# Seven products of 256 columns in place of eight for the three feed-forward parts

## The reference, cut to what matters

```python
def swiglu_ffn(x, w_gate, w_up, w_down):
    return (jax.nn.silu(x @ w_gate) * (x @ w_up)) @ w_down
...
        x = layer_norm(DN_ALPHA * x + 0.5 * swiglu_ffn(x, ffn1_wg[i], ffn1_wu[i], ffn1_wd[i]),
                       ln1_g[i], ln1_b[i])
...
        h = rmsnorm(x, norm_mlp_w[l]) * (1.0 + scale2) + shift2
        x = x + gate2 * (jnp.square(jax.nn.relu(h @ w_up[l])) @ w_down[l])
```

## Time and profile before

| | |
|---|---|
| three runs, median | 5414.38 us |
| profiled execution | 5398.97 us, span 5397.2 us, mean granted clock 0.969 |
| TensorE busy | 5041.7 us, 93% |
| VectorE busy | 1668.1 us, 31% |
| ScalarE busy | 872.1 us, 16% |
| matmuls of the pairs (line 261) | 3465.9 us busy, 8016 records |
| weight loads of the same | 1524.9 us busy |

### The profile page before, as it was taken

One profiled execution on the slowest core, in us unless ns is written; L12 is line 12 of the kernel. 1 busy time (PEld: TensorE's weight loads), 2 busy tenths in 40 slices (PEclk: granted clock), 3 DMA queues, 4 the chain that ended last, 5 costly groups with the idle time before them and its releaser, 6 DMA issues.

```text
span 5397.2 us, 48490 instructions
## 1 busy us (share of the span) xinstructions
PE 5041.7 (93%) x21092; PEld 2886.4 (53%) x21092; DVE 1668.1 (31%) x2883; ACT 872.1 (16%) x1483; POOL 146.7 (3%) x228
## 2 busy tenths in 40 slices
PE   8999997989999998999999999899999788888988
PEld 3444444775564443466555444344444677778843
DVE  1211875440211001462442100221010555555501
ACT  0001023121021000311221100010001333233211
POOL 0000000000000000000000000000000111111000
PEclk9999998999999999899999999999999899999999
DMA  5432441003222222111111222222221000000021
GB/s 199 150 111 53 70 66 45 1 3 92 86 79 70 72 78 68 47 39 63 39 41 54 68 73 78 70 70 70 71 69 56 3 1 1 1 1 1 17 89 39
DMA packets 284883, 311.14 MB, mean 58 GB/s; under 512 B 7168, under 2 KB 277632, under 8 KB 281472
## 3 DMA queue, kind: packets, MB, share of 16 engines
q1 hardware_dynamic: 284672, 308.04, 19.2%
HBM read 305.92 MB, written 2.10 MB: 57 GB/s over the span
## 4 chain that ended last, share of the span: by engine, by line
PE 51%; DVE 3%; ACT 2%; issue 0%; DMA 0%; SPq 0%; DVEq 0%; ACTq 0%
PE ps L261 31%; PE ps L579 4%; PE ps L592 2%; PE ps L566 1%; PE ps L2417 1%; PE ps L1727 1%; PE ps L306 1%; PE ps L342 1%; PE ps L2435 1%; PE ps L599 1%; PE ps L2656 1%; PE ps L1446 1%; PE ps L2178 1%; PE ps L1435 1%; PE ps L2348 0%; PE ps L2337 0%
## 5 line engine op out<-in xcount | busy, mean ns | idle before, releaser
L261 PE MATMUL ps<-main,w 128*128 128x512 f32 (+1 forms) x8016 | 3465.9, 593 | 69.6 <-DMA w<-in_ffn_wg 19.0
L261 PEld LDWEIGHTS ps<-main,w 128*128 128x128 f32 x8016 | 1524.9, 191 | 1933.6 <-issue 1905.6
L579 PE MATMUL ps<-main,w 128*128 128x128 f32 x1536 | 219.3, 290 | 4.3 <-DVE main L2521 2.5
L579 PEld LDWEIGHTS ps<-main,w 128*128 128x128 f32 x1536 | 197.2, 201 | 16.5 <-issue 6.8
L535 DVE SCALAR_TENSOR_TENSOR main<-main,ps 128x512 f32<-128x512 f32 x44 | 30.3, 688 | 553.0 <-PE ps L261 553.0
L592 PE MATMUL ps<-main 128*128 128x128 f32 x1440 | 195.6, 292 | 2.4 <-DVE main L638 2.4
L488 DVE SCALAR_TENSOR_TENSOR main<-main,params_sb 128x512 f32<-128x512 f32 x256 | 192.5, 752 | 9.1
L592 PEld LDWEIGHTS ps<-main 128*128 128x128 f32 x1440 | 184.4, 207 | 10.6 <-issue 7.5
L612 ACT COPY main<-ps 128x512 f32<-128x512 f32 x180 | 105.5, 586 | 516.4 <-PE ps L566 516.4
L566 PE MATMUL ps<-consts_sb,main 128*128 128x128 f32 x944 | 141.1, 276 | 7.0 <-DVE main L622 7.0
L546 DVE SCALAR_TENSOR_TENSOR main<-main,ps 128x512 f32<-128x512 f32 x32 | 22.0, 688 | 399.9 <-PE ps L261 399.9
(11 more groups left out here) (417 smaller groups left out, 3853.6 us busy)
## 6 DMA issues: line engine op xcount, KB each, us to landing
w<-in_w_in SPq DMA_DIRECT2D x58, 1024.0 KB, 6.5
w<-in_e_w_in SPq DMA_DIRECT2D x28, 1024.0 KB, 5.0
main<-in_ada_w SPq DMA_DIRECT2D x24, 1024.0 KB, 9.3
w<-in_ffn_wg SPq DMA_DIRECT2D x22, 1024.0 KB, 5.2
w<-in_ffn_wu SPq DMA_DIRECT2D x22, 1024.0 KB, 5.3
w<-in_o_w_in SPq DMA_DIRECT2D x20, 1024.0 KB, 5.4
w<-in_ffn_wd SPq DMA_DIRECT2D x16, 1024.0 KB, 4.8
w<-in_w_up SPq DMA_DIRECT2D x16, 1024.0 KB, 5.4
```

Of the source, the lines that this page charges most:

```text
L261: i = pe.mm(PS[b][:, 0:n], wv[:, k, f * 128:(f + 1) * 128], g.X(kg + k), start=kg + k == 0, stop=kg + k == g.nk - 1)
L579: t = pe.mm(one(PS[b], i), one(MT, i), one(Dm, i), start=True, stop=True)
```

## The change

The three parts use the scheme of Strassen in Winograd's form. A pair of output features by a pair of inner tiles is a 2x2 block matrix of 128x128 weights, and two inner tiles by two halves of the tokens a 2x2 block matrix of 128x256 data. Instead of eight block products of 256 columns (done before as four of 512) there are seven, each summed over the n = 4 pairs of inner tiles of one weight buffer (n = 3 in the last group of the ffn's down). What is multiplied and how the results are combined needs sums:

- four sums of weights for each buffer, two steps ahead (`dve_seven_weights`), in two sets of buffers;
- four sums of data for each pair of inner tiles, once for x and once for the hidden tiles (`dve_halves`, three instructions each);
- four instructions on the results of each step (`dve_seven_out`), out of four banks, beside one copy by ScalarE.

A step is now one weight buffer: the down products are no longer summed in PSUM over all inner tiles, but added to X step by step. The first pair of gate and of the MLP's up stays as it was. Silu runs on two tiles at once in SBUF, the MLP's ReLU and square are one instruction of VectorE. The modulation rows have three buffers rather than seven and stand one behind each step (three behind the first). U2 has one set of 16 tiles.

```diff
     w_landed = [ctx.enter_context(nc.semaphore(f"w_landed{i}")) for i in range(4)]
-    mod_landed = [ctx.enter_context(nc.semaphore(f"mod_landed{i}")) for i in range(7)]
     PS = [ctx.enter_context(nc.psum_tensor(f"ps{i}", [128, 512], F32))[:, :] for i in range(8)]
-    banks, weights = Turns(8), Turns(4)
...
+    def seven_room(g, j, kg):
+        n, (S, first, _, _) = min(8, g.nk - kg) // 2, g.seven
+        w = wbuf[weights.of.get((g, j, kg), 0)][:, 0:n * 512].rearrange("p (m e f n) -> p m e f n", e=2, f=2, n=128)
+        i = sets.of.get((g.name, j, kg), 0)
+        parts = [S[i](q)[:, 0:n * 128].rearrange("p (m n) -> p m n", n=128) for q in range(4)]
+        return n, [[w[:, :, e, f, :] for e in range(2)] for f in range(2)], parts, first[i]
+    def pe_seven(pe, g, j, kg=0):
+        step = (g.name, j, kg)
+        weights.take(g, j, kg)
+        sets.take(*step)
+        n, w, S, _ = seven_room(g, j, kg)
+        _, _, XS, key = g.seven
+        into = [banks.take("seven", i, *step) for i in range(4)]
+        def product(q, i, half, weight, x):
+            b, before = into[i]
+            if before:
+                pe.wait_ge(*at("out", *before))
+            for m in range(n):
+                t = pe.mm(PS[b][:, 256 * half:256 * half + 256], weight[:, m, :], x(m), start=m == 0, stop=m == n - 1)
+            t.then_inc(pe.inc(sem["pe", "dense"], "mm", f"seven {q}", *step), 1)
...
+        def own(e, half):
+            return lambda m: g.X(kg + 2 * m + e)[:, 256 * half:256 * half + 256]
+        def sums(q):
+            return lambda m: XS[kg // 2 + m][q // 2][:, 256 * (q % 2):256 * (q % 2) + 256]
...
+        pe.wait_ge(*at("w", g.name, j, kg))
+        for m in range(0, 2 * n, 2):
+            pe.wait_ge(*at(*g.ready, kg + m))
+        product(1, 0, 0, w[0][0], own(0, 0))
+        yield
+        for m in range(1, 2 * n, 2):
+            pe.wait_ge(*at(*g.ready, kg + m))
+        product(2, 1, 0, w[0][1], own(1, 0))
+        yield
+        for m in range(n):
+            pe.wait_ge(*at("halves", *key, kg // 2 + m))
+        product(4, 3, 1, w[1][1], sums(3))
+        yield
+        pe.wait_ge(*at("sums", *step))
+        product(6, 1, 1, S[1], sums(2))
+        pe.also("w used", *step)
+        yield
+        product(5, 2, 0, S[0], sums(0))
+        yield
+        product(7, 2, 1, S[2], sums(1))
+        yield
+        product(3, 3, 0, S[3], own(1, 1))
+        yield
+    def act_seven(a, g, j, kg=0):
+        step = (g.name, j, kg)
+        before = sets.before.get(step)
+        if before:
+            a.wait_ge(*at("out", "seven", 1, *before))
+        a.wait_ge(*at("mm", "seven 1", *step))
+        _, _, _, first = seven_room(g, j, kg)
+        a.copy(first, bank("seven", 0, *step)[:, 0:256]).then_inc(
+            a.inc(sem["act", "dense"], "out", "seven", 0, *step), 1)
+    def dve_seven_weights(v, g, j, kg=0):
+        s, step = sem["dve", "dense"], (g.name, j, kg)
+        before = sets.before.get(step)
+        if before:
+            v.wait_ge(*at("mm", "seven 3", *before))
+        v.wait_ge(*at("w", *step))
+        _, ((a11, a12), (a21, a22)), S, _ = seven_room(g, j, kg)
+        v.tt(S[0], a21, a22, ADD).then_inc(v.inc(s, "sum 0", *step), 1)
+        v.tt(S[2], a21, a11, SUB).then_inc(v.inc(s, "sum 2", *step), 1)
+        v.wait_ge(*at("sum 2", *step))
+        v.tt(S[1], S[2], a22, ADD).then_inc(v.inc(s, "sum 1", *step), 1)
+        v.wait_ge(*at("sum 1", *step))
+        v.tt(S[3], a12, S[1], SUB).then_inc(v.inc(s, "sums", *step), 1)
+    def dve_halves(v, key, X, XS, m, ready):
+        s = sem["dve", "dense"]
+        x = X.ap[:, 2 * m:2 * m + 2, :].rearrange("p a (h n) -> p (a h) n", n=256)
+        a, b = (t.rearrange("p (q n) -> p q n", n=256) for t in XS[m])
+        v.wait_ge(*at(*ready, 2 * m))
+        v.wait_ge(*at(*ready, 2 * m + 1))
+        v.tt(a, x[:, 1:2, :].broadcast_to([128, 2, 256]), x[:, 0:4:3, :], SUB).then_inc(
+            v.inc(s, "halves 1", *key, m), 1)
+        v.wait_ge(*at("halves 1", *key, m))
+        v.tt(b[:, 0, :], x[:, 3, :], a[:, 0, :], SUB).then_inc(v.inc(s, "halves 2", *key, m), 1)
+        v.wait_ge(*at("halves 2", *key, m))
+        v.tt(b[:, 1, :], x[:, 2, :], b[:, 0, :], SUB).then_inc(v.inc(s, "halves", *key, m), 1)
+    def dve_seven_out(v, g, j, kg, out):
+        s, step = sem["dve", "dense"], (g.name, j, kg)
+        _, _, _, first = seven_room(g, j, kg)
+        c = out.rearrange("p (c n) -> p c n", n=256)
+        b = [bank("seven", i, *step).rearrange("p (h n) -> p h n", n=256) for i in range(4)]
+        two = lambda x: x.unsqueeze(1).broadcast_to([128, 2, 256])
+        v.wait_ge(*at("out", "seven", 0, *step))
+        v.wait_ge(*at("mm", "seven 6", *step))
+        v.tt(c[:, 0:4:3, :], two(first), b[1], ADD).then_inc(v.inc(s, "out", "seven", 1, *step), 1)
+        v.wait_ge(*at("out", "seven", 1, *step))
+        v.wait_ge(*at("mm", "seven 7", *step))
+        v.tt(c[:, 1:3, :], two(c[:, 3, :]), b[2], ADD).then_inc(v.inc(s, "most", *step), 1)
+        v.wait_ge(*at("most", *step))
+        v.tt(c[:, 3, :], c[:, 2, :], b[2][:, 0, :], ADD).then_inc(v.inc(s, "out", "seven", 2, *step), 1)
+        v.wait_ge(*at("mm", "seven 3", *step))
+        v.wait_ge(*at("out", "seven", 2, *step))
+        v.tt(c[:, 1:3, :], c[:, 1:3, :], b[3], ADD).then_inc(v.inc(s, "out", "seven", 3, *step), 1)
...
+    def ffn_steps(name):
+        g, u, d = FFN[name]
+        both = [(p, j, 0) for j in range(0, 22, 2) for p in (g, u)]
+        return both[1:] + [(d, j, kg) for j in range(0, 8, 2) for kg in (0, 8, 16)]
+    def pe_ffn(pe, name, aside=()):
+        run(pe_pair(pe, FFN[name][0], 0))
+        for q, step in enumerate(ffn_steps(name)):
+            run(pe_seven(pe, *step))
+            for what in aside[0:3] if q == 0 else aside[q + 2:q + 3]:
...
         after(a, *before)
-        for f in range(22):
+        g, u, d = FFN[name]
+        for f in range(2):
             a.wait_ge(*at("mm", name + " g", f))
             a.act(H1(f), bank(name + " g", f), ACT.Silu).then_inc(a.inc(s, "out", name + " g", f), 1)
+        for p, j, kg in ffn_steps(name):
+            act_seven(a, p, j, kg)
+            if p is g:
+                a.wait_ge(*at("out", "seven", 3, g.name, j, 0))
+                a.act(H1.ap[:, j:j + 2, :], H1.ap[:, j:j + 2, :], ACT.Silu).then_inc(
+                    a.inc(s, "out", name + " g", j + 1), 1)
         a.fence(name)
...
-        dve_residual(v, name + " d", ready, total)
+        g, u, d = FFN[name]
+        steps = ffn_steps(name)
+        for m in range(4):
+            dve_halves(v, (name + " x",), X, FX, m, ready)
+        for step in steps[0:2]:
+            dve_seven_weights(v, *step)
+        for _ in range(3):
+            next(aside, None)
+        used = None
+        for q, (p, j, kg) in enumerate(steps):
+            if p is g:
+                dve_seven_out(v, g, j, 0, H1.ap[:, j:j + 2, :].rearrange("p a b -> p (a b)"))
+            else:
+                if used:
+                    v.wait_ge(*at(*used))
+                dve_seven_out(v, p, j, kg, FO)
+                v.wait_ge(*at("out", "seven", 3, p.name, j, kg))
+            if p is u:
+                v.wait_ge(*at("out", name + " g", j + 1))
+                v.stt(H1.ap[:, j:j + 2, :], H1.ap[:, j:j + 2, :], 0.5, FO.rearrange("p (a b) -> p a b", b=TOK), MUL,
+                      MUL).then_inc(v.inc(s, "out", name + " u", j), 1)
+                v.also("out", name + " u", j + 1)
+                used = ("out", name + " u", j)
+            if p is d:
+                done = ("out", name + " d") if kg == 16 else ("part", name + " d", kg)
+                for f in (j, j + 1):
+                    r = FO[:, TOK * (f - j):TOK * (f - j) + TOK]
+                    if kg:
+                        v.wait_ge(*at("part", name + " d", kg - 8, f))
+                        t = v.tt(X(f), X(f), r, ADD)
+                    else:
+                        v.wait_ge(*at(*ready, f))
+                        t = v.stt(X(f), X(f), ALPHA, r, MUL, ADD)
+                    t.then_inc(v.inc(s, *done, f), 1)
+                    used = (*done, f)
+                    if kg == 16:
+                        dve_total(v, total, f, X, ("out", name + " d"))
+            if q + 2 < len(steps):
+                dve_seven_weights(v, *steps[q + 2])
+            next(aside, None)
+            if 18 <= q < 21:
+                v.wait_ge(*at("mod", q + 3))
+                for m in ((0, 1), (2, 3), (4, 5, 10, 6, 7, 8, 9))[q - 18]:
+                    dve_halves(v, (name + " h",), H1, FH, m, ("out", name + " u"))
         v.fence(name)
...
-                t = v.stt(acc, MW[m % 7], cact[:, k:k + 1], acc, MUL, ADD)
+                t = v.stt(acc, MW[m % 3], cact[:, k:k + 1], acc, MUL, ADD)
             else:
-                t = v.ts(acc, MW[m % 7], cact[:, k:k + 1], None, MUL)
...
+    G_down = [Gemm(f"down{i}", io["w_down_2"][2048 * i:2048 * i + 2048, :], 0, 8, 16, U2, ("relu2", i),
```

(35 more changed lines are left out.)

108 lines of the change are left out of this document (55 added, 53 removed).

## The result

The change makes the kernel faster: four runs of it have a median of 5260.75 us (5247.91 to 5261.3) beside 5415.76 us for the kernel before, a ratio of 0.9708 with the 95% interval [0.969, 0.9726]. In a second comparison, four other runs gave 5254.19 against 5414.15 us, 0.9707 [0.9693, 0.9722]. The forecast was 5265.7 us in a range of 5252 to 5290. The sign, the size and the range hold; the gain was some 6 to 11 us larger than forecast. The experiments show that this surplus arises outside the three changed parts, in the main as a side effect on the PSUM banks that a later matmul is given.

A forecast was written before the change was run, and what follows sets the result against it. TensorE's time alone was taken to bound the three feed-forward parts. Shorter records gain 155.6 us, tails cost 6.9, so 148.7 us come off the median of 5414.38: 5265.7 us, range 5252 to 5290.

The forecast's parts named there:

- The rate of a short product: TensorE in the three parts: a 256-column record takes 0.2159 us against 0.4291 for 512 columns; gross gain 155.6 us.
- The edge row: Rival: short products run at line 261's 0.2188 us a record, +15 us, 5281 us in all; chance 0.06.
- VectorE beside it: Three parts: VectorE's turns, 9.0 us at most in ffn1, fit beside TensorE's 12.09 us steps, or 9.07 in short ones.
- the tight place: Turn of gate/up to down in ffn1: the fifth halves are ready 0.35 us before need; cost 0, at most about 2 us.
- The start and SP's queue: Start of ffn1: step 1's weights, behind three modulation rows, land by 33 us, and three row buffers suffice; cost 0.
- The tails: Behind each part's last matmul: 2.1 us more in each ffn and 2.7 in the MLP, 6.9 us in all.
- The sum: Whole kernel: 155.6 us gained less 6.9 lost in tails, 148.7 us net, giving 5265.7 us against the median.
- The lower end of the range: Whole kernel: 5252 us, with tails at nothing (-6.9) and the spread of the runs (-4).
- Late turns: Rival: VectorE's waits cost more, or starts and turns lose 3 to 10 us each; about 5290 us; chance 0.13.
- Nothing gained: Rival: weight loads hold a 256-column record at 0.245 us, half the old step; 5421 us; chance 0.01.
- The slower one: Rival: VectorE becomes the bound and TensorE's stops lose its clock, 3.1 us a step; 5567 us; chance 0.03.
- my largest turn: VectorE's longest turn in ffn1, with one modulation row on top: 9.0 us at most.

The follow-up runs named there:

- four more additions a turn: Full change with four dependent 512-element additions on VectorE behind each step's weight sums, into an unread tile: 5261.99 us, 0.9721 of the kernel before.
- the short tails: Full change with each part's last step reordered, product 3 last and the next norm's totals gathered ahead of it: 5243.56 us, 0.9688 of the kernel before.
- the banks are put back: Full change with the PSUM bank counter moved on by six ahead of the convolution's layer norm, so its mean takes bank 7 again: 5272.49 us, 0.9739.
- the kernel with eight additions: Full change with eight dependent 512-element additions on VectorE behind each step's weight sums: 5366.39 us, 0.9913 of the kernel before.
- the kernel with twelve: Full change with twelve dependent 512-element additions on VectorE behind each step's weight sums: 5628.77 us, 1.0398 of the kernel before.
- the kernel with eight products of 256 columns: Kernel before, with ffn gate and up and the MLP's up cut into 256-column halves, no sums and no seven products: 5407.27 us, 0.9992.
- the kernel with the MLP alone: Seven products in the MLP only, both feed-forwards and the modulation rows as in the kernel before: 5360.5 us, 0.99 of the kernel before.

## Why the prediction was right

**The rate of a short product** was the step on which all hung, and it holds. TensorE's timeline at the start of ffn1 after:

```profile
19.08 15.46 PE L262 MATMUL ps<-main,w 128*128 128x512 f32 x32 [19.08 <-DMA w<-in_ffn_wg]
34.38 5.34 PE L338 MATMUL ps<-main,w 128*128 128x256 f32 x24
39.56 7.07 PE L338 MATMUL ps<-main 128*128 128x256 f32 x32
46.47 5.34 PE L338 MATMUL ps<-main,w 128*128 128x256 f32 x24
```

From the first group at 34.38 to the next like it at 46.47 are 12.09 us for 56 records, 0.2159 each: the value taken from the earlier trace rows. The edge row was edge, not rate. The choice between the two rows was right for the reason given: one was an unbroken stretch, the other a mean with its bursts' edges in it. The weight loads have the 190 ns of the earlier trace rows.

**VectorE beside it.** The timeline of VectorE at the turn of ffn1 follows the chain of the prediction instruction by instruction:

```profile
288.40 0.69 DVE L425 TENSOR_TENSOR main<-main,ps 128x512 f32<-128x512 f32 x1 [0.51 <-PE ps L338]
289.12 1.23 DVE L684 SCALAR_TENSOR_TENSOR main<-main 128x1024 f32<-128x1024 f32 x1
290.27 0.69 DVE L387 TENSOR_TENSOR main<-w 128x512 f32<-128x512 f32 x1
290.87 0.69 DVE L388 TENSOR_TENSOR main<-w 128x512 f32<-128x512 f32 x1
291.59 0.69 DVE L390 TENSOR_TENSOR main<-main,w 128x512 f32<-128x512 f32 x1
292.31 0.69 DVE L392 TENSOR_TENSOR main<-w,main 128x512 f32<-128x512 f32 x1
292.92 2.34 DVE L868 SCALAR_TENSOR_TENSOR main<-main 128x2048 f32<-128x2048 f32 x1
295.30 0.69 DVE L401 TENSOR_TENSOR main<-main 128x512 f32<-128x512 f32 x1
296.02 0.43 DVE L404 TENSOR_TENSOR main<-main 128x256 f32<-128x256 f32 x1
296.49 0.42 DVE L406 TENSOR_TENSOR main<-main 128x256 f32<-128x256 f32 x1
296.83 0.69 DVE L401 TENSOR_TENSOR main<-main 128x512 f32<-128x512 f32 x1
```

Line 425 is the last add of a step's output, 684 the product of up and gate, 387 to 392 the weight sums, 868 the modulation row, 401 to 406 one pair's halves. The two weight sums that don't need each other start 0.60 us apart, the dependent ones 0.72. One pair's halves take 1.53 us from start to start (295.30 to 296.83) where I had 1.61, so the fifth is ready at 303.0, and TensorE's third product of that step starts at 303.74: a slack of 0.7 us rather than 0.35. It was right to cost the turn at nothing, and right to name it as the tight place: with four more additions a turn the stop of 6 us stands exactly there. That only turn 20 had been followed didn't matter here, because turns 18 and 19 with their two pairs of halves still fit. The views with steps and broadcasts cost what plain ones do (0.69 and 0.42).

**The start and SP's queue.** TensorE starts at 19.08 rather than 18.96 us, and its first product of 256 columns follows at 34.38. The weights of step 1, behind three modulation rows, landed at 32.3 us, against my bound of 33. The rows land in a median of 4.9 us instead of the 9.3 of the earlier trace rows, perhaps because with three buffers fewer of them stand in the same rush; no run tests that.

**The tails** came as worked out, and with one thing I had not costed. The mean's matmul in ffn1, ffn2 and the MLP after:

```profile
424.99 2.04 PE L456 MATMUL ps<-tmp,consts_sb 128*128 128x512 f32 x2 [3.67 <-DVE tmp L476]
...
2025.93 2.05 PE L456 MATMUL ps<-tmp,consts_sb 128*128 128x512 f32 x2 [3.67 <-DVE tmp L476]
...
3297.76 2.05 PE L456 MATMUL ps<-tmp,consts_sb 128*128 128x512 f32 x2 [5.12 <-DVE tmp L483]
```

3.67, 3.67 and 5.12 us stand where 1.60, 1.67 and 2.40 stood, +2.1, +2.0 and +2.7: 6.8 us beside the 6.9 of the sum. What was missing: behind the longer stop the granted clock is 0.50 (window of 425.00 to 427.05 us), and the pair of matmuls itself takes 2.05 us where it took 1.10 in the ffns and 1.48 in the MLP. With the short tails it is 1.12 again in ffn1, at clock 1.00.

**The sum.** 148.7 us were expected, 150.0 measured in the three stages, and 141.7 in the whole time once the banks are put back (5414.15 - 5272.49). The whole change shows 155.0 and 160.0 in its two comparisons. So the forecast stands between: its steps were right for the three parts, and what it left out altogether is that the number of banks a step takes shifts the user of every later bank. This term was about -12 us in the stage (-16.7 and -18.3 in the medians of the two kernels that move the counter alone). I had costed the new banks only by whether they come free in time inside the changed parts, and took for granted that what follows would stand as before. That the whole time came so near the forecast is in part luck: in the two profiles the -7.8 us of the first mixers and the +9.7 of the second, neither of them forecast, nearly cancel.

The lower end of the range is 3 us too low for its own terms: 5265.7 - 6.9 - 4 is 5254.8, not 5252. The first comparison lies above either figure, the second, 5254.19, between the two.

**The rivals.** Late turns: none. The edge row: gone with the rate. Nothing gained: gone with it. The slower one: its first half, VectorE as the bound, is real, and I had put its point at 1.35 times my largest turn, 12.09 us. TensorE does stop from there, but the kernel is not slower than before from there: with turns of 13.8 us it is still 0.9913. Its second half, 1.73 us a step for lost clock on top, doesn't hold in a row of such steps. With stops of 0.66 and 1.92 us the clock stays at 1.00 between 100 and 300 us, unlike between the short bursts of the earlier trace rows. With stops of 2.0 to 2.6 us most steps lose 1.6 to 1.8 us, but these lie under VectorE's turn. I had added the two losses where only the larger counts; only at a single longer stop (5.97 us, four additions) do both add up. The Trainium skill (TensorE: Matmul & The Clock Gate, "A second HAM failure mode: psum-queue depth-cycling") warns of just this pattern, groups of matmuls that cycle through banks with small idle times between. The change has seven groups a step but no idle times, and its clock in ffn1 is 1.00; the kernel with eight additions has real stops and keeps 1.00 over eleven of them, until 302.30 us; the kernel with twelve shows the swing.

**What stays open.** The mixers of block 2 take 858.3 or 858.4 us in the profiles of before and of the kernel with eight products of 256 columns, and 863 to 868 in the others, with equal idle time of TensorE (59 to 61 us). The difference goes with the granted clock of single stretches: the same work at 1.00 in the kernel before (first) and at 0.89 in the kernel with the MLP alone (second), windows of 30 us.

```profile
2570.00:2600.00 30.00, 25.70 (x299) 16.51 (x298) 16.53 (x32) 8.39 (x15) 0.00 (x0) 1.00 0.12 37
```

```profile
2576.00:2606.00 30.00, 25.70 (x280) 16.95 (x281) 14.17 (x27) 8.49 (x15) 0.00 (x0) 0.89 0.12 36
```

This isn't plain scatter. The second half of the stage, from the mean's matmul at 2540.0 us of before on, takes 453.8 us in the first two, 459.4 and 459.5 in the two kernels that move the counter of the banks by hand, and 461.2 to 461.4 in all eight that have the seven products in the feed-forwards and leave the counter alone. There the counter stands where it stood before, two further and four further. But the kernel with the MLP alone, whose counter hasn't moved, has 462.6, so the counter isn't shown to be the cause. The last stage, too, takes 1948 to 1962 us without a pattern. So a single profile settles a difference of a few microseconds in an unbroken part, but not one of 10 in the mixers; for the banks it took thirteen profiles and the medians.

## What to carry to other kernels

Where TensorE is busy without a break, its time for a piece of work is the count of records by the rate of an unbroken stretch of the same shape, and VectorE's new work is free as long as the chain of a turn, followed in order and with its bunches, ends before TensorE asks. Carry the lateness of one turn into the next: here two turns ahead of the tight one made a stop of 2.2 us one of 6.0. Count what follows the last product by itself: rearranging the last step's results took 8 us off the three parts, beside the 150 of the change. When a change takes another number of slots out of a ring shared by the whole kernel, look up who follows whom at every later wait; a shift by two was worth as much as some optimisations, and it can be had without the change.

## What the runs showed of the hardware

- A fp32 matmul of 256 columns with weights of 128x128 keeps half the time of one with 512 (0.2159 us a record, two records each) for as long as it lasts: over 400 us, beside a VectorE that is busy 66% of them and reads the same weight buffers.
- The granted clock stayed at 1.00 while TensorE stopped 0.66 and 1.92 us in turn, once in each step of 12.5 us of work, ten times; behind the next stop of 1.92 us it fell, and 32 records took 8.86 rather than 7.17 us. With stops of 2.0 to 2.6 us in nearly every step it was 0.93, and the 16 records behind most of them took 5.2 to 5.4 rather than 3.62 us. Between the short bursts of the earlier trace rows, stops of 1.3 to 1.5 us had come with 0.74.
- A clock lost in this way cost nothing where VectorE's turn was the bound in every step (two steps of 33.4 us, twice 13.8 + 2.9), and came on top of the stop where TensorE stopped once: 5.97 us, then 8 records in 3.46 rather than 1.89 us.
- After a stop of 3.67 us the next two records of 512 columns took 2.05 us at a granted clock of 0.50, after one of 2.40 us 1.48, after one of 1.07 or 1.60 us 1.12 and 1.10.
- The bank that one matmul of the layer norm happened to be given cost 12 us in its stage: 25.83 us of waiting for ScalarE's copy, against 5.67.
